# First layer, modulation tiles 25 to 47: from GpSimd's sums to direct products on TensorE

## What is computed

```
def modulation(cond, w_mod, b_mod):
    return jnp.split(jax.nn.silu(cond) @ w_mod + b_mod, 6, axis=-1)

for i in range(DEPTH):                                   # DEPTH = 2
    sh1_l, sc1_l, gt1_l, sh2_l, sc2_l, gt2_l = modulation(c, w_mod[i], b_mod[i])
    sh1_c, sc1_c, gt1_c, sh2_c, sc2_c, gt2_c = modulation(c_ctx, w_mod[i], b_mod[i])
    h = x * (1 + sc1) + sh1
    o = even_mixer(h) if i % 2 == 0 else odd_mixer(h)    # two attentions, or a differential one
    x = layer_norm(ALPHA * x + gt1 * o)
    h = x * (1 + sc2) + sh2
    x = layer_norm(ALPHA * x + gt2 * conv_ffn(h))
```

## Time and profile before

| what | value |
|---|---|
| median of 3 runs | 3366.11 us (3364.45 to 3366.71) |
| span of the profiled execution, first to last instruction | 3365.9 us |
| TensorE busy | 3107.7 us, 92% of the span |
| VectorE busy | 1731.8 us, 51% |
| ScalarE busy | 970.2 us, 29% |
| GpSimd busy | 752.8 us, 22% |
| mean granted TensorE clock | 0.938 of full speed |

### The profile page before, as it was taken

How to read it: one execution, slowest core, us unless ns; L and a number is a source line. 1 busy time by engine, 2 the same in 40 slices (tenths; PEclk the granted TensorE clock), 3 DMA queues, 4 the chain that set the end, 5 groups by cost and what they waited for, 6 DMA issues and landing times.

```text
span 3365.9 us, 37638 instructions
## 1 busy us (share of the span) xinstructions
PE 3107.7 (92%) x14864; PEld 2446.9 (73%) x14864; DVE 1731.8 (51%) x2927; ACT 970.2 (29%) x1533; POOL 752.8 (22%) x850
## 2 busy tenths in 40 slices
PE   6989999989999998998988999878897899999999
PEld 5876556868888886776676888654566678778887
DVE  5267466353333435426746645479985643343333
ACT  1223344142212213214524323320124422232222
POOL 2568544017475510100001000035410000000000
PEclk9986899989999999999989999988876899999999
DMA  5211000202333321210011233211121013322332
GB/s 203 82 57 43 30 32 26 66 35 88 110 125 129 119 68 46 75 58 18 1 44 63 88 107 96 80 44 38 50 73 38 1 57 100 94 71 96 97 100 81
DMA packets 67341, 238.16 MB, mean 71 GB/s; under 512 B 7392, under 2 KB 10592, under 8 KB 66400
## 3 DMA queue, kind: packets, MB, share of 16 engines
q1 hardware_dynamic: 66880, 234.19, 21.1%
q10 hardware_dynamic: 288, 1.57, 0.1%
HBM read 233.64 MB, written 2.10 MB: 70 GB/s over the span
## 4 chain that ended last, share of the span: by engine, by line
PE 76%; DVE 13%; ACT 4%; POOL 3%; issue 3%; DMA 0%; ACTq 0%; DVEq 0%; SPq 0%; POOLq 0%
PE PS L514 74%; PE PS L680 1%; DVE stat L1742 1%; ACT Y L1236 1%; POOL MPROD L1554 1%; DVE WS L1632 1%; DVE Y L1776 1%; POOL MPROD L1555 1%; DVE Y L2117 1%; ACT Y L1156 1%; PE PS L1097 1%; DVE Y L1775 1%; DVE Y L2114 1%; DVE Y L2113 1%; POOL X L1534 1%
## 5 line engine op out<-in xcount | busy, mean ns | idle before, releaser
L514 PE MATMUL PS<-HS,WS 128*128 128x512 f32 (+1 forms) x7104 | 1503.6, 373 | 78.8 <-DVE HS L1652 44.3
L514 PEld LDWEIGHTS PS<-HS,WS 128*128 128x128 f32 x7104 | 1250.5, 193 | 339.1 <-issue 95.6
L1632 DVE TENSOR_TENSOR WS<-W,WS 128x1024 fp32r<-128x1024 f32 (+2 forms) x358 | 421.5, 1179 | 611.6 <-ACT WS L1173 610.6
L1173 ACT ACTIVATE WS<-W 128x1024 fp32r<-128x1024 f32 (+2 forms) x358 | 351.1, 983 | 923.9 <-PE PS L514 805.6
L514 PE MATMUL PS<-Y 128*64 128x128 f32 (+8 forms) x2240 | 497.4, 385 | 93.1 <-DVE Y L2127 39.5
L514 PE MATMUL PS<-YS,WS 128*128 128x512 f32 (+1 forms) x2688 | 561.6, 370 | 3.5 <-DVE YS L2237 3.5
L514 PEld LDWEIGHTS PS<-YS,WS 128*128 128x128 f32 x2688 | 470.5, 189 | 91.2 <-DVE YS L2237 3.9
L514 PEld LDWEIGHTS PS<-Y 128*64 128x64 f32 (+4 forms) x2240 | 312.0, 180 | 245.4 <-issue 93.8
L1554 POOL TENSOR_TENSOR MPROD<-W,silu_c 128x512 f32<-128x512 f32 x204 | 219.2, 1075 | 275.0 <-DMA W<-in_weights 260.1
L1156 ACT ACTIVATE Y<-PS 128x768 f32<-128x768 f32 (+5 forms) x181 | 119.5, 661 | 377.0 <-PE PS L514 322.2
L1534 POOL TENSOR_SCALAR X<-X 128x768 f32<-128x768 f32 (+1 forms) x32 | 65.1, 2061 | 643.2 <-DVE HS L1652 643.2
(11 more groups left out here) (248 smaller groups left out, 2534.4 us busy)
## 6 DMA issues: line engine op xcount, KB each, us to landing
W<-in_weights SPq DMA_DIRECT2D x396, 512.0 KB, 3.5
Y<-in_early SPq DMA_DIRECT2D x4, 2048.0 KB, 14.6
W<-in_weights SPq DMA_DIRECT2D x24, 256.0 KB, 2.6
X<-in_x SPq DMA_DIRECT2D x1, 3072.0 KB, 28.1
W<-in_weights SPq DMA_DIRECT2D x24, 128.0 KB, 2.1
Y<-in_ssm ACTq DMA_DIRECT2D x1, 1024.0 KB, 7.2
out<-X SPq DMA_DIRECT2D x1, 1024.0 KB, 4.5
C<-in_consts SPq DMA_DIRECT2D x1, 948.5 KB, 34.3
```

The costliest lines, as they stand in the source:

```text
L514: return pe.matmul(out, lhsT, rhs, start=first, stop=last)
L1173: act.activation(WS[:, n % R_RING, 0, 0:f], W[:, c % W_RING, 0:f], ACT.Copy)\
L1632: tt(WS[:, n % R_RING, 1, 0:f], W[:, c % W_RING, 0:f], WS[:, n % R_RING, 0, 0:f].bitcast(F32), ALU.subtract).then_inc(weights_split, 1)
```

## The change

`by_gpsimd` now gives GpSimd, of the first layer, only the odd tiles between 16 and 25. Tiles 25 to 47 become direct. GpSimd's loop for tiles 40 to 47 goes. The places of the tiles in TensorE's and VectorE's order stay as they are, as does the order of the loads; what releases a ring place of these 23 tiles is now the tile's own matmuls.

```diff
 def by_gpsimd(layer, n):
 
-    return n >= (SUMMED if layer == 0 else 16) or (n % 2 == 1 and (layer == 1 or n > EARLY))
+    if layer == 0:
+        return EARLY < n < SUMMED and n % 2 == 1
+    return n >= 16 or n % 2 == 1
...
             pool.wait_ge(shared_key_spread, value("shared_key_spread"))
-            for n in range(40, 48):
-                mod_products(0, n)
             for n in range(48):
```

## The result

| | median of 17 runs | range of the runs |
|---|---|---|
| before | 3366.06 us | 3357.68 to 3369.72 |
| changed | 3371.52 us | 3368.56 to 3379.78 |

The medians are 5.5 us apart. The ratio, which is estimated from all runs, is 1.0022, 95% interval 1.0014 to 1.0029: slower by 7.4 us, between 4.7 and 9.8. Between runs of one kernel lie 11 or 12 us, so a single profile can't tell such a difference. The changed kernel's profiled span, 3375.5 us, is 9.6 us above that of before; its execution was one of the slower ones, 6 us above the median.

What follows compares the result with a forecast made beforehand. TensorE was taken to bound the window attention, much of the time at its lower clock. Window attention 39.1 + low-rank attention 17.0 - VectorE's 3 = 53.1 us on 3365.9 gave 3419 us, slower by 1.6%, range 3395 to 3445.

Steps and rivals of the forecast that it cites:

- the head of the window attention: Per head: first-unit tile -0.2 us, fourth-unit tile at the lower clock +2.8, later clock rise +2.3; together +4.9 us.
- the later rise: Window attention, behind a fourth-unit tile: clock rises later, inside units five, six and next first; 5 us low, +2.3 us.
- 39.1 - 3: Window attention: 39.1 us summed over its heads, less 3 us for VectorE running without GpSimd beside it.
- VectorE's relief: Window attention: VectorE faster without GpSimd's sums, counted only where TensorE waits for ScalarE; 3 us off, between 0 and 4.6.
- First head, +7.5: Window attention's first head, low from its start: two tiles at the lower clock, +2.5 and +2.7, later rise +2.3.
- Second head, +4.9 + 2.4: Window attention's second head: +4.9 like the others, +2.4 because it ran high before and will now fall too.
- Low-rank attention, 17.0: 8 direct tiles x 1.34 = 10.7 us of work, plus +6.3 for clock falls behind 4 of 8.
- Transfers and GpSimd's other work at nothing: Later-freed ring places covered by four places of tiles; GpSimd's copy and second-layer sums behind other waits; both cost nothing.
- Rival 1: Window attention's clock holds, as idle waits alone caused falls: +3 us, less a further 16, so 3353 us; chance 0.07.
- Rival 2: Only the work is added, clock falls and rises stay where they were: +19, 3385 us; chance 0.22.
- Rival 3: Window attention stays at the low clock altogether: +89 less 1, 3454 us; chance 0.12.
- Rival 4: Nothing measurable, because the added 31 us of tile work hides in waits; chance 0.04.

Runs made afterwards that it cites:

- the table: Window attention, two small matmuls or direct tiles, GpSimd idle or busy: 3351.7 and 3364.6 us with small matmuls, 3371.5 and 3386.4 with direct tiles.
- the one with 13 sums: Kernel before with all 23 tiles still by GpSimd but spread, 10 in the window attention and 13 in the low-rank one: 3359.61 us, ratio 0.9972.
- The moved tile: Kernel with direct tiles at fourth units, GpSimd summing the rest, its direct tile moved to the fifth unit: 3367.11 us, ratio 1.0004 to the kernel before.
- the idle kernel with small matmuls: Changed kernel with two one-column matmuls on constants in place of tiles 25 to 39, GpSimd idle: 3351.67 us, ratio 0.9948 to the kernel before.

## Why the prediction was wrong

**The account by the runs.** A path from before to the changed kernel in medians: the waits -9.5, the low-rank attention direct +8.7, the load -13.0, the tiles +19.9. Sum +6.1, measured +5.5. This agreement is no test: the steps are differences of neighbouring kernels, so their sum is the whole difference whatever each step is, but for the chips. With each kernel against the one before on its own chip they are -9.5, +6.6, -13.0 and +21.3. Each holds its own part of the clock, and each is uncertain by some 5 us. What does test the steps is that load and tiles each came out alike in their two measurements in the table. The low-rank attention, 10.8 us in its own run, is 6.6 to 9 us here.

**The step that failed** is the head of the window attention: "The tile there replaces wait and small matmuls: 1.84 - 2.06 = -0.2 us, and the clock falls as before." It did not fall as before. From the third head on it never fell behind a first-unit tile, and with it went what hung on it: the fourth-unit tile "at the lower clock: 3.55 - 0.73 = +2.8 us" took 1.84 us, and the later rise "+2.3" had nothing to rise from. Heads three to seven, forecast at +4.9 each, averaged -1.4. The window attention, forecast at 39.1 - 3, gave -2.8 in its own runs. The error was to take the 2.1 us in front of a fall, seen in one profile, for its cause, and to leave all that surrounds it as it was. The same change took GpSimd's load away, and the surroundings ran another way. But the load explains only its 13 to 17 us of the 39. With the load put back, the window attention was 11.4 us longer than before in the profile (201.5 against 190.1 from first scores to last transposes), not 39, and of the six fourth-unit tiles behind the first head only two took 3.41 us; the others took 1.84 to 2.09. So even then the tile did not stand at the lower clock in each head and did not push the rise back.

**The terms one by one.**
- *GpSimd's waits*: I had them in the heads as 2.06 us for 1.84. Their removal is worth 9.5 us, between 5.7 and 14.5, where they last 9.2. The head's term is not contradicted, and not measured more closely than that.
- *VectorE's relief, 3 us, between 0 and 4.6*: it is 13 to 17 us. The upper bound came from the waits for ScalarE, and this is where it broke: a wait for GpSimd's sum and the low clock hid the chain over VectorE and ScalarE. In the four kernels with GpSimd as busy and its waits gone or nearly gone those for ScalarE are 8.3 to 12.7 us instead of 4.6. In the changed kernel they are 14.0 us although VectorE's operations are shorter, as its clock is higher and TensorE arrives earlier. A faster VectorE may also shorten the thin stretches, so that part of the gain comes back through the clock: 0.74 to 0.84 between busy and idle GpSimd is 36 us less at the lower level, at the prediction's 0.46 some 17 us by estimate, against 13 to 15 measured. The other pair, 0.82 to 0.85, gives 5 by this reckoning against 13.0. So how the gain divides between clock and shorter waits is not settled.
- *The rule on the shared interfaces* (the Trainium skill, GPSIMD Engine Reference, section 1): I had cited it and then held its effect down. The rows of both kernels with GpSimd busy agree with it (776 and 805 ns against 487). Holding it down to 3 us was 10 to 14 us of the 39 by which the window attention was forecast too long.
- *A direct tile's own work, 1.3 us at the higher clock*: right, in both attentions.
- *First head, +7.5*: +4.3. Its tiles took 3.57 and 3.41 us as forecast; the later rise did not come. *Second head, +4.9 + 2.4*: +3.3; it did fall, as said. *Last head, -0.2*: -2.9, for it ran high from its start.
- *Low-rank attention, 17.0*: the 10.7 us of work are there (runs: 10.8, and 7 to 9 by the other pair; profile 12.5), while 4 falls of 1.6 us were forecast and 2 came. The mechanism was right, the clock's term of 6.3 mis-sized: in the profile 12.5 - 10.7 = 1.8 us.
- *Transfers and GpSimd's other work at nothing*: nothing speaks against it.
- *Not in the sum*: the fall at the end of the low-rank attention, which the kernel before has too, was 3.4 us shorter in the changed profile, and what follows that attention 2.3 us shorter.

**The rivals.** Rival 1's heads came closest: without its further 16 us it says -7.6 for the window attention and 10.7 for the low-rank one, 3369 us. Third to seventh head have -1.4 on average where it had -1.5. Its condition is only half fulfilled, since from the third head on the clock holds behind first units and falls behind every second fourth one; and its last 16 us were not to be had. It had 0.07 and should have had more: "for it: the falls follow waits". Rival 2, +19, is nearest in time among those with a whole sum, and its low-rank and first-head terms are right; the heads behind the first should have come to -6.5, not +6. Rival 3, like the forecast, had the clock falling further where it rose. Rival 4 had the time, though not the reason: it stood for a change within 0.2%, 7 us, at a chance of 0.04, and the medians are 0.16% apart, the ratio 0.22%. But the added work did not hide in waits. The tiles cost 20 to 25 us in the window attention and 7 to 12 in the low-rank one, and what stands against them is the relief and the waits. That two gains and two costs of this size could nearly cancel was given no chance of its own, and this is why 0.04 was too little; that they did so to 5 us is luck.

**The rule on idle gaps.** I had set the Trainium skill (TensorE: Matmul & The Clock Gate, "HAM oscillation") aside on the row at 820 us. By it the direct tiles should cost no clock, and for the window attention that is nearly what happened with GpSimd idle: 0.84 with tiles and 0.85 without. With GpSimd busy it is 0.74 and 0.82, which is a little more than one profile can be off. The rule does not cover the rows either, though. In the low-rank attention only the kernels with direct tiles, and the one with 13 sums, have a fall inside it, and the one at 565.6 us began 2.8 us behind a tile with no idle time before it. The moved tile's 24 us at 0.57 with TensorE busy throughout began behind a direct tile. Ahead of that last tile TensorE had waited for ScalarE, so gap and tile are not separated there. What decides whether the clock falls at a given place stays open; that it alternates from head to head is seen and not explained.

## What to carry to other kernels

When a change takes work off an engine that shares something with another, price that relief by a run with the load put back unread, not by the waits that stand in the profile: waits name only what ends last now. Don't extrapolate the clock from the operation just ahead of a fall; if the change touches what surrounds it, give the clock both ways a real chance. And a choice between two engines need not be all or nothing: half of the tiles each way took away the waits and half of the load for half of the price, and beat both kernels, while the move of the tiles that had waited for nothing (the low-rank attention's) was the whole loss. Nor is a place without waits free for more work: compare each stage's own length, as the spread sums gained 15.7 us in one attention and lost 8.4 in the other. A list of differences between neighbouring kernels always adds up; only a cell measured twice tests it.

## What had not been expected of the hardware

- Half of GpSimd's load (72 us in 180) cost TensorE nothing that the runs can show, the whole of it (130 us) 13 to 17 us.
- Dense matmuls without use, 32.5 us of them, cost nothing on balance ahead of the waits, and the clock was higher with them (0.72 to 0.88, ratio 0.9999).
- In the changed kernel the clock fell 2.2 to 3.3 us after the start of a direct tile in the window attention and 2.2 and 2.8 us after it in the low-rank one (tiles at 440.54 and 562.82 us), with TensorE busy for 4.00 of 4.00 us in the stretches shown. How long it stayed low differed by place: 3.4 us in the low-rank attention, 6.7 us where dense units follow, 13.6 us behind the second head's first unit and, with the moved tile, 20.6 us, though TensorE was busy all the while. It also falls in this stage without any direct tile (the idle kernel with small matmuls).
- Beside GpSimd's sums VectorE's normalisation took 767 to 805 ns instead of 487 and its one-column product 291 to 351 instead of 150, while its reduction for the row maxima (691 or 692) and its reciprocal (164) did not change.
- Identical code in the window attention read a clock of 0.77 in one profile and 0.82 in another.
